# A two-layer transformer block on one core: each change of norm goes by halves of the tokens, and most residual additions go to GpSimd

## The chip, the core and the metric

One core of a Trainium2 chip runs one program in one launch. The time is device microseconds from start to end of that program. The engines are TensorE (PE, matrix products; PEld is its loading of weights), VectorE (DVE), ScalarE (ACT), GpSimd (POOL) and SyncE (SP, which issues loads). They run side by side, each through its own queue in order, and wait for one another only through semaphores. TensorE writes to PSUM, eight banks of 128 x 512 numbers of 32 bits; VectorE and ScalarE read PSUM, and GpSimd works on SBUF.

## What is computed

The input x has 512 tokens of 1024 features. Two layers follow one another. The first mixes tokens by retention (with states of a context of 256 tokens) and by a Fourier transform, and then has a feed-forward part with a convolution along rows of 64 tokens. The second has a causal convolution beside stick-breaking attention, and a gated feed-forward part. Around every part stands the same pattern:

```python
h = modulate(rms_norm(x, g_mix_pre[layer]), sh_a, sc_a)
mix = token_mixer(h, ...)
x = x + gt_a * rms_norm(mix, g_mix_post[layer])
h_ffn = modulate(rms_norm(x, g_ffn_pre[layer]), sh_f, sc_f)
ffn = conv_ffn(h_ffn, ...)
x = x + gt_f * rms_norm(ffn, g_ffn_post[layer])
```

rms_norm divides a token by the root of the mean of its squares. So where one part hands over to the next, each token needs first the mean square of the part's output y, then, with the new x, the mean square of x. The program has three such changes of norm inside it (after the first mixer, after the first feed-forward part, after the second mixer). The last norm, before the output, is made in another way and is not touched.

## The kernel before

**Layout.** Activations lie feature-major: a tile is 128 features by 512 tokens, and a tensor of 1024 features has KT = 8 tiles. All products are in two pieces: weights and activations are split into a rounded part (WH, hH) and the remainder (WL, hL), and `mm3` makes three matmuls of them. Weights come as chunks of 128 x 2048 (SP loads `raw`, ScalarE rounds it to WH in `split_hi`, VectorE makes the remainder WL in `split_lo`), in three slots; the load of chunk c waits until chunk c-3 has been used.

**A stage's end.** `out_phase` (first and third change) and `down_phase` (second) compute the eight tiles of y, two by chunk. For every tile ScalarE takes two squares from PSUM (of y, and of y times the gain gp), and VectorE writes y times gain to yT and its product with x, and adds these three up in `sums` (`out_tile`: four operations, L1164 to L1176). For the last tile VectorE instead makes the product and yT straight from PSUM.

**The change of norm.** `late_stats` adds, on TensorE, the last tile's squares and product to the sums over features (`token_sums`, with a matrix of ones), ScalarE takes the inverse root (`y_root`), VectorE works out from the three sums what the mean square of the new x will be (`boundary`), ScalarE takes its inverse root, and TensorE spreads each root over all partitions (`spread`, L1526). Between these steps `keep_running` (L1780) issues 13 matmuls whose result is not used. Then, for each of eight tiles, VectorE scales y (L1183), adds it to x (L1187), multiplies by gain and root (L1210), ScalarE adds the shift and rounds (hH, L646), and VectorE takes the remainder (hL, L1216). `lead` on TensorE takes these tiles as they come, for two chunks at once: eight matmuls on hH and four on hL each. `third` does the third chunk after that.

**Order.** Nothing is scheduled by a program: each engine's instructions stand in the order written in its block, and the semaphores are counted.

## Time and profile before

| | us |
|---|---|
| time, median of 3 runs (lowest to highest) | 1351.64 (1349.67 to 1352.57) |
| the profiled execution: time / span | 1350.7 / 1348.9 |
| TensorE busy in the span | 1331.0 (99%) |
| VectorE busy | 901.1 (67%) |
| ScalarE busy | 527.0 (39%) |
| GpSimd busy | 84.0 (6%) |
| granted clock of TensorE, mean | 0.999 |

Busy times overlap in a pipelined engine: matmuls of 128 x 512 last 0.39 us each and start 0.227 us apart. So what TensorE costs is read from the starts of its instructions, and what it idles from the numbers in brackets. A time in a timeline is the start from the span's beginning; the number behind it is how long the instruction took.

### The profile page before, as it was taken

Reading aid. Unit: us, or ns where it says so; the run is one execution under the profiler, and the core shown is the slowest. Engines: PE = TensorE matmul, PEld = TensorE weight load, DVE = VectorE, ACT = ScalarE, POOL = GpSimd, SP = SyncE. Lnnn points to the kernel's source line nnn. Section 1 sums busy time; section 2 is a strip of 40 time slices with the busy share of each in tenths; the row PEclk is TensorE's granted clock in tenths of the full one; section 3 lists DMA queues with packets and bytes.
Section 4 is the critical chain, followed back from the end, with each engine's and each line's share of the span. In section 5 each row is a group of like instructions: output and inputs, shape, how many; then the busy total and the mean of one; then the engine's idle time right before and its main releaser. Section 6 shows DMA issues by size and latency. Waiting matters only on the chain.

```text
span 1348.9 us, 15748 instructions
## 1 busy us (share of the span) xinstructions
PE 1331.0 (99%) x6467; PEld 1078.8 (80%) x6467; DVE 901.1 (67%) x1126; ACT 527.0 (39%) x747; POOL 84.0 (6%) x148
## 2 busy tenths in 40 slices
PE   7999999999999999999999999999999999999998
PEld 4799688778888888887888777778878888888886
DVE  4787878988777777678758799766775333332224
ACT  4552444344344443222422666774333222222112
POOL 0000001000000001000000100000001220000000
PEclk9999999999999999999999999999999999999999
DMA  9543046325445455664122211112224332224321
GB/s 387 193 139 127 17 155 218 126 78 176 166 160 201 172 185 179 213 212 162 71 94 97 91 63 63 63 63 95 95 81 139 115 113 98 94 95 162 109 104 63
DMA packets 32887, 176.47 MB, mean 131 GB/s; under 512 B 4128, under 2 KB 4400, under 8 KB 17840
## 3 DMA queue, kind: packets, MB, share of 16 engines
q1 hardware_dynamic: 19440, 128.78, 26.7%
q0 software_dynamic: 13376, 46.69, 10.7%
q8 instruction: 51, 0.84, 0.2%
q14 instruction: 20, 0.16, 0.0%
HBM read 171.26 MB, written 4.20 MB: 130 GB/s over the span
## 4 chain that ended last, share of the span: by engine, by line
PE 90%; DVE 5%; ACT 2%; DMA 1%; issue 1%; SPq 0%; DVEq 0%; ACTq 0%
PE bank L1473 27%; PE bank L1475 26%; PE bank L1474 26%; PE bank L1813 2%; PE bank L1814 2%; PE bank L1819 2%; PE bank L1678 1%; DMA adaf<-ada 1%; DVE WL L829 1%; PE bank L2018 1%; PE bank L1988 1%; PE bank L2006 1%; DVE sums L1172 1%; PE bank L2005 1%; DMA raw<-weights 0%
## 5 line engine op out<-in xcount | busy, mean ns | idle before, releaser
L1473 PE MATMUL bank<-hH,WH 128*128 128x512 f32 x992 | 390.0, 393 | 0.9 <-DVE WL L829 0.6
L829 DVE TENSOR_TENSOR WL<-raw,WH 128x2048 fp32r<-128x2048 f32 x103 | 234.5, 2279 | 232.0 <-ACT WH L371 232.0
L1475 PE MATMUL bank<-hH,WL 128*128 128x512 f32 x992 | 386.4, 390 | 0.0
L1474 PE MATMUL bank<-hL,WH 128*128 128x512 f32 x992 | 386.2, 389 | 0.0
L371 ACT ACTIVATE WH<-raw 128x2048 fp32r<-128x2048 f32 x106 | 201.7, 1905 | 245.8 <-DMA raw<-weights 245.8
L1473 PEld LDWEIGHTS bank<-hH,WH 128*128 128x128 f32 x992 | 186.3, 188 | 42.5 <-issue 3.3
L1475 PEld LDWEIGHTS bank<-hH,WL 128*128 128x128 f32 x992 | 186.2, 188 | 39.6
L1474 PEld LDWEIGHTS bank<-hL,WH 128*128 128x128 f32 x992 | 186.3, 188 | 37.6 <-issue 0.2
L858 DVE SCALAR_TENSOR_TENSOR ada_acc<-ada_half,csil,ada_acc 128x1024 f32<-128x1024 f32 x70 | 89.7, 1281 | 6.0 <-DMA ada_half<-ada_later 3.5
L1305 DVE SCALAR_TENSOR_TENSOR cacc<-uT,vec,cacc 128x511 f32<-128x511 f32 (+29 forms) x120 | 83.3, 759 | 0.0
L334 POOL DMA_DIRECT2D ada_half<-ada_later x80 | 42.6, 533 | 574.9 <-DVE ada_acc L858 341.0
L1473 PE MATMUL bank<-GH,WH 128*128 128x512 f32 x176 | 68.8, 391 | 0.0
L1474 PE MATMUL bank<-GL,WH 128*128 128x512 f32 x176 | 68.5, 389 | 0.0
L1475 PE MATMUL bank<-GH,WL 128*128 128x512 f32 x176 | 68.5, 389 | 0.0
L1473 PE MATMUL bank<-WH,GH 128*128 128x512 f32 x176 | 68.5, 389 | 0.0
L1474 PE MATMUL bank<-WL,GH 128*128 128x512 f32 x176 | 68.5, 389 | 0.0
L1475 PE MATMUL bank<-WH,GL 128*128 128x512 f32 x176 | 68.5, 389 | 0.0
L805 ACT ACTIVATE GH<-tB 128x512 fp32r<-128x512 f32 x22 | 14.0, 634 | 86.8 <-DVE tB L1444 86.8
L1263 DVE SCALAR_TENSOR_TENSOR tB<-bank,vec,tB 128x504 f32<-128x504 f32 x22 | 16.4, 743 | 40.8 <-ACT tB L659 40.7
L659 ACT ACTIVATE tB<-bank,vec 128x512 f32<-128x512 f32 x22 | 17.2, 780 | 67.0 <-PE bank L1475 67.0
L1813 PE MATMUL bank<-hH,WH 128*128 128x512 f32 x96 | 37.6, 392 | 1.8 <-ACT hH L646 1.8
L1473 PEld LDWEIGHTS bank<-GH,WH 128*128 128x128 f32 x176 | 33.0, 188 | 7.1 <-issue 0.2
(333 smaller groups left out, 2080.8 us busy)
## 6 DMA issues: line engine op xcount, KB each, us to landing
raw<-weights SPq DMA_DIRECT2D x108, 1024.0 KB, 4.9
ada_half<-ada_later POOLq DMA_DIRECT2D x80, 512.0 KB, 4.0
adaf<-ada SPq DMA_DIRECT2D x8, 1024.0 KB, 20.0
xT<-x_t SPq DMA_DIRECT2D x4, 512.0 KB, 6.1
x_rows<-xB POOLq DMA_DIRECT2D x32, 64.0 KB, 2.2
x_tok<-x_rows POOLq DMA_DIRECT2D x1, 2048.0 KB, 10.7
out_t<-x_tok SPq DMA_DIRECT2D x8, 256.0 KB, 2.0
ctxT<-ctx_t SPq DMA_DIRECT2D x1, 1024.0 KB, 28.2
```

Of the source, the lines that this page charges most:

```text
L334: pool.dma_start(ada_half[:, a % 2, :], ada_later[a]).then_inc(ada_in[a % 2], 16)
L371: A(WH[:, slot, 0:width], raw[:, slot, 0:width], ACT.Copy).then_inc(s.hi_done, 1)
L659: A(tmp[:, j, :], bank[2 * (t % 3) + x][:, :], ACT.Identity, bias=v("cb", x * FT + t), scale=v("cw", 2 * FT + x * FT + t)).then_inc(s.conv ...
L829: TT_(WL[:, slot, 0:width], raw[:, slot, 0:width], WH[:, slot, 0:width], sub).then_inc(s.lo_done, 1)
L858: ins = STT(ada_acc[:, :], w, c_col, ada_acc[:, :], mult, add)
L1305: STT(cacc[:, k, shift:L], uT[:, k, 0:L - shift], w, cacc[:, k, shift:L], mult, add)\
L1473: mm(o, lh, rh, start=start, stop=False, skip_group_check=skip)
L1474: mm(o, lh, rl, start=False, stop=False, skip_group_check=skip)
L1475: return mm(o, ll, rh, start=False, stop=stop, skip_group_check=skip)
L1813: mm(o, wh, hH[:, k, :], start=(k == 0), stop=False)
L1814: mm(o, wl, hH[:, k, :], start=False, stop=False)
L1819: ins = mm(bank[banks[j] + x][:, :], wh, hL[:, k, :], start=False, stop=(k == KT - 1))
```

## The change

The last two tiles of y (6 and 7) and the first four tiles of the next stage's input are each taken in two halves of 256 tokens. `TURNS` lists the twelve turns: tiles 0 to 3 of the first half, 0 to 3 of the second, then 4 to 7 whole. `closing` on TensorE makes tile 6 and tile 7 on the first half, then both on the second half, and puts the statistics and the spreading of the first half between the products of the second; `lead` starts with the first half and has the statistics of the second half between its products. `keep_running` is gone. ScalarE now takes one square of tiles 6 and 7 and writes y times gain itself; the square with gain comes from the weights of the summing (gp_last has two columns). The split of the second leading chunk is made in two halves (`lead_hi`, `lead_lo`). VectorE makes the addition to x for turns 0, 4 and 8 only; the other nine of each change are made by GpSimd (`residual`). The additions of squares before a stage's last statistics are five instead of six, and the sums are closed at tile 5 instead of tile 6. For the first change `mod_sum` moves ahead of tile 6. PSUM banks are handed out differently, and the three chunks of a column of w_down hold 8, 6 and 8 blocks instead of 8, 8 and 6.

```diff
-Y_BANKS = {0: (2, 3, 0, 1), 1: (2, 3, 0, 1), 2: (0, 1, 2, 3), 3: (2, 3, 0, 1)}
+Y_BANKS = {0: (2, 3, 0, 1), 1: (0, 1, 2, 3), 2: (0, 1, 2, 3)}
+UP_BANKS = (2, 0, 4)
...
+FIRST, SECOND, BOTH = slice(0, HALF), slice(HALF, L), slice(0, L)
+TURNS = [(k, FIRST) for k in range(4)] + [(k, SECOND) for k in range(4)] + [(k, BOTH) for k in range(4, KT)]
+NT = len(TURNS)
+OWN_ADDS = (0, 4, 8)
+DOWN_AT = (0, 8, 14, FT)
...
+            def residual(m):
+
+                for i, (k, ts) in enumerate(TURNS):
+                    if i not in OWN_ADDS:
+                        pool.wait_ge(s.y_scaled, NT * m + i + 1)
+                        nc.gpsimd.tensor_tensor(xT[:, k, ts], xT[:, k, ts], yT[:, k, ts], add).then_inc(s.x_new, 1)
...
                 pool.dma_start(ada_half[:, a % 2, :], ada_later[a]).then_inc(ada_in[a % 2], 16)
+                if a == STEPS_UP + 1:
+                    residual(0)
+
+            residual(1)
...
+            def change(m, c):
+
+                def lead_hi(half):
+                    slot = (c + 2) % SLOTS
+                    at = slice(CH // 2 * half, CH // 2 * half + CH // 2)
+                    if half == 0:
+                        act.wait_ge(raw_in[slot], 16 * ((c + 2) // SLOTS) + 16)
+                    A(WH[:, slot, at], raw[:, slot, at], ACT.Copy).then_inc(s.hi_done if half else s.hi_half, 1)
+
+                def square(n, half):
+                    ts, b = TURNS[4 * half][1], bank[Y_BANKS[m][2 + n]]
+                    act.wait_ge(s.mm_done, done(c, 2 * half + n, 4))
+                    if half == 0:
+                        act.wait_ge(s.sq_added, 5 * m + 4 + n)
+                    A((scratch, odd_sq[m])[n][:, 0, ts], b[:, ts], ACT.Square).then_inc(s.yy_ready, 1)
+
+                def gained(n, half):
+                    ts, b = TURNS[4 * half][1], bank[Y_BANKS[m][2 + n]]
+                    ins = A(yT[:, 6 + n, ts], b[:, ts], ACT.Identity, scale=gp[:, 6 + n:7 + n])
+                    ins.then_inc(s.bank_free if half else s.zz_ready, 1)
...
+                def rounded(i):
+                    k, ts = TURNS[i]
+                    at = SHIFT_AT[m + 1] + k
+                    act.wait_ge(s.norm_mul, KT + NT * m + i + 1)
+                    A(hH[:, k, ts], tmp1[:, k % 4, ts], ACT.Identity, bias=mod[:, at:at + 1]).then_inc(s.h_hi, 1)
+
+                square(0, 0)
+                gained(0, 0)
+                lead_hi(0)
+                square(1, 0)
+                gained(1, 0)
+                y_root(0)
+                square(0, 1)
+                x_root(0)
+                gained(0, 1)
+                rounded(0)
+                square(1, 1)
+                gained(1, 1)
+                rounded(1)
+                y_root(1)
+                rounded(2)
+                rounded(3)
+                x_root(1)
+                rounded(4)
+                rounded(5)
+                lead_hi(1)
+                rounded(6)
+                rounded(7)
+                split_hi(c + 3)
+                for i in range(8, NT):
...
-                if n == KT - 1:
-                    b = bank[Y_BANKS[m][n % 4]]
-                    dve.wait_ge(s.yy_ready, m * KT + n + 1)
-                    STT(last_xy[m][:, :], b[:, :], gp[:, n:n + 1], xT[:, n, :], mult, mult).then_inc(s.xy_ready, 1)
-                    TS(yT[:, n, :], b[:, :], gp[:, n:n + 1], None, mult).then_inc(s.bank_free, 1)
-                    return
-                dve.wait_ge(s.zz_ready, m * (KT - 1) + n + 1)
+                dve.wait_ge(s.zz_ready, 8 * m + n + 1)
...
+            def change(m, c, free0):
+
+                def lead_lo(half):
+                    slot = (c + 2) % SLOTS
+                    at = slice(CH // 2 * half, CH // 2 * half + CH // 2)
+                    if half:
+                        dve.wait_ge(s.hi_done, c + 3)
+                    else:
+                        dve.wait_ge(s.hi_half, 2 + m + 1)
+                    TT_(WL[:, slot, at], raw[:, slot, at], WH[:, slot, at], sub)\
+                        .then_inc(s.lo_done if half else s.lo_half, 1)
...
+                def product(n, half):
+                    ts = TURNS[4 * half][1]
+                    to = scratch[:, 1, ts] if n == 0 else last_xy[m][:, ts]
+                    if half:
+                        dve.wait_ge(s.bank_free, free0 + 7 + n)
+                    else:
+                        dve.wait_ge(s.zz_ready, 8 * m + 7 + n)
+                    TT_(to, yT[:, 6 + n, ts], xT[:, 6 + n, ts], mult).then_inc(s.xy_ready, 1)
...
+                def rest(i):
+                    k, ts = TURNS[i]
+                    at = SHIFT_AT[m + 1] + k
+                    dve.wait_ge(s.h_hi, KT + NT * m + i + 1)
+                    STT(hL[:, k, ts], tmp1[:, k % 4, ts], mod[:, at:at + 1], hH[:, k, ts], add, sub)\
+                        .then_inc(s.h_lo, 1)
+
+                product(0, 0)
+                lead_lo(0)
+                product(1, 0)
...
+                mean_a(0)
+                mean_b(0)
+                dve.wait_ge(s.y_spread, 2 * m + 1)
                 scale_y(0)
+                add_x(0)
                 scale_y(1)
-                add_x(0)
+                product(0, 1)
                 dve.wait_ge(s.gm_ready, m + 1)
-                dve.wait_ge(s.x_spread, m + 2)
...
+                dve.wait_ge(s.x_spread, 2 * m + 2)
+                norm(0)
+                scale_y(2)
+                rest(0)
+                norm(1)
+                scale_y(3)
+                product(1, 1)
+                rest(1)
+                norm(2)
+                mean_a(1)
+                rest(2)
+                norm(3)
+                mean_b(1)
+                rest(3)
+                dve.wait_ge(s.y_spread, 2 * m + 2)
+                scale_y(4)
+                add_x(4)
+                scale_y(5)
+                dve.wait_ge(s.x_spread, 2 * m + 3)
+                norm(4)
+                scale_y(6)
+                rest(4)
+                norm(5)
+                scale_y(7)
+                rest(5)
+                norm(6)
+                lead_lo(1)
+                rest(6)
+                scale_y(8)
+                norm(7)
+                add_x(8)
+                rest(7)
+                scale_y(9)
+                norm(8)
+                dve.wait_ge(s.bank_free, free0 + KT)
+                scale_y(10)
+                rest(8)
+                norm(9)
+                scale_y(11)
+                rest(9)
...
-                pe.wait_ge(s.sq_added, 6 * m + 6)
-                token_sums(4, sums[m][:, 0, :], True, False)
-                token_sums(5, sums[m][:, 1, :], True, False)
-                pe.wait_ge(s.xy_added, 6 * m + 6)
-                token_sums(6, sums[m][:, 2, :], True, False)
-
-            def keep_running(m, times):
-
-                c, still = ((C_UP, mixH[:, 7, :]), (C_U, GH[:, 10, :]), (C_UP2, q2L[:, 3, :]))[m]
-                for _ in range(times):
-                    mm(bank[7][:, :], wblock(c, 0, 0, P)[0], still, start=True, stop=True)
-
-            def late_stats(m):
...
-                have((C_UP, C_U, C_UP2)[m])
+                pe.wait_ge(s.sq_added, 5 * m + 5)
+                token_sums(6, sums[m][:, 0, :], True, False)
                 pe.wait_ge(s.mod_read, (2, 5, 6)[m])
-                keep_running(m, 2)
-
-                pe.wait_ge(s.yy_ready, (m + 1) * KT)
-                token_sums(4, odd_sq[m][:, 0, :], False, True).then_inc(s.ystat_done, 1)
+                token_sums(7, sums[m][:, 1, :], True, False, at=P)
+                pe.wait_ge(s.xy_added, 5 * m + 5)
+                token_sums(6, sums[m][:, 2, :], False, False, at=2 * P)
+
+            def late_squares(m, half):
+
+                qs = (2 * half, 2 * half + 1)
+                pe.wait_ge(s.yy_ready, 10 * m + 8 + 2 * half)
+                token_sums(6, scratch[:, 0, :], False, False, blocks=qs)
...
+            def spread_half(b, src, half):
+
+                ps = slice(64 * half, 64 * half + 64)
+                for q in (2 * half, 2 * half + 1):
+                    ins = mm(bank[b][:, P * q:P * q + P], lift[ps, q:q + 1].to_broadcast([64, P]), src[ps, :],
+                             start=True, stop=True, skip_group_check=True)
+                return ins
+
...
+            def spread_x(m, half):
+
+                pe.wait_ge(s.xroot_ready, 2 * m + half + 2)
+                if half:
+                    pe.wait_ge(s.norm_mul, KT + NT * m + 4)
+                spread_half(5, xroot, half).then_inc(s.x_spread, 1)
...
+            def closing(m, c, ks, src_h, src_l):
+
+                def part(n, half, a, b):
+                    ts, o = TURNS[4 * half][1], bank[Y_BANKS[m][2 + n]]
+                    for x in range(a, b):
+                        kb, k = ks[x]
+                        wh, wl = wblock(c, kb, P * n, P * n + P)
+                        ins = mm3(o[:, ts], wh, wl, src_h[:, k, ts], src_l[:, k, ts],
+                                  m != 1 and half == 0 and x == 0, x == KT - 1, True)
+                    if b == KT:
+                        ins.then_inc(s.mm_done, step(2 * half + n, 4))
+
+                part(0, 0, 0, KT)
+                part(1, 0, 0, 4)
+                early_stats(m)
+                part(1, 0, 4, KT)
+                pe.wait_ge(s.zz_ready, 8 * m + 7)
+                part(0, 1, 0, 3)
+                late_squares(m, 0)
+                part(0, 1, 3, 6)
...
+                late_products(m, 0)
+                spread_y(m, 0)
+                part(0, 1, 6, KT)
+                pe.wait_ge(s.zz_ready, 8 * m + 8)
+                part(1, 1, 0, 5)
+                spread_x(m, 0)
+                part(1, 1, 5, KT)
+
+            def lead(m, c, banks, freed):
+
+                def with_hi(i, js=(0, 1)):
...
+                have(c)
+                pe.wait_ge(s.bank_free, freed - 2)
+                with_hi(0, (0,))
+                with_lo(0, (0,))
+                late_squares(m, 1)
+                with_hi(1, (0,))
+                pe.wait_ge(s.lo_half, 2 + m + 1)
+                pe.wait_ge(s.bank_free, freed)
+                with_hi(0, (1,))
+                with_lo(0, (1,))
+                with_hi(1, (1,))
+                with_lo(1)
+                late_products(m, 1)
+                spread_y(m, 1)
+                with_hi(2)
+                with_lo(2)
+                with_hi(3)
+                spread_x(m, 1)
+                with_lo(3)
+                for i in range(4, NT):
+                    if i == 8:
+                        have(c + 1)
+                    with_hi(i)
+                    with_lo(i)
...
-                        if m == 0 and t == KT - 1:
-                            mod_sum(1, 2)
...
+                if m == 0:
+                    mod_sum(1, 2)
+                closing(m, c0 + 3, order, src_h, src_l)
...
-                        ks = [(k, 8 * j + k) for k in range(min(8, FT - 8 * j))]
+                        ks = [(k, DOWN_AT[j] + k) for k in range(DOWN_AT[j + 1] - DOWN_AT[j])]
```

**TensorE's queue at the end of the first mixer.** `sums`, `odd_sq`, `last_xy` and `scratch` hold the squares and products, `rstd,lift` is the spreading of a root. Before:

```order
L1519 MATMUL bank<-sums_163,ones 32x128 x12
L1473 MATMUL bank<-mixH,WH 128x512
L1474 MATMUL bank<-mixL,WH 128x512
L1475 MATMUL bank<-mixH,WL 128x512
L1780 MATMUL bank<-mixH,WH 128x512 x2
L1519 MATMUL bank<-odd_sq_161,ones 32x128 x4
L1519 MATMUL bank<-odd_sq_161,gp_last 32x128 x4
L1780 MATMUL bank<-mixH,WH 128x512 x2
L1519 MATMUL bank<-last_xy_162,ones 32x128 x4
L1526 MATMUL bank<-rstd,lift 128x128 x4
L1780 MATMUL bank<-mixH,WH 128x512 x4
```

After, from the first half's late statistics to its first spreading:

```order
L1604 MATMUL bank<-mixH,WL 128x256
L1648 MATMUL bank<-scratch,ones 32x128 x2
L1648 MATMUL bank<-odd_sq_161,ones 32x128 x2
L1648 MATMUL bank<-scratch,gp_last 32x128 x2
L1648 MATMUL bank<-odd_sq_161,gp_last 32x128 x2
...
L1604 MATMUL bank<-mixH,WL 128x256
L1648 MATMUL bank<-scratch,ones 32x128 x2
L1648 MATMUL bank<-last_xy_162,ones 32x128 x2
L1929 MATMUL bank<-rstd,lift 128x128 x2
L1602 MATMUL bank<-mixH,WH 128x256
```

The sums and the spreading now stand between products of 256 columns instead of between matmuls without use.

**VectorE's queue before tile 6 of the first mixer.** Before (tile 5, then tile 6):

```order
L1164 TENSOR_SCALAR yT<-bank,gp 128x512
L1167 TENSOR_TENSOR last_xy_162<-yT,xT 128x512
L1172 TENSOR_TENSOR sums_163<-sums_163,odd_sq_161 128x1024
L1176 TENSOR_TENSOR sums_163<-sums_163,last_xy_162 128x512
L1164 TENSOR_SCALAR yT<-bank,gp 128x512
```

After (tile 5, then the first half of tile 6):

```order
L941 TENSOR_TENSOR mod<-bank,vec 128x16
L1220 TENSOR_SCALAR yT<-bank,gp 128x512
L1223 TENSOR_TENSOR last_xy_162<-yT,xT 128x512
L1228 TENSOR_TENSOR sums_163<-sums_163,odd_sq_161 128x1024
L1232 TENSOR_TENSOR sums_163<-sums_163,last_xy_162 128x512
L1253 TENSOR_TENSOR scratch<-yT,xT 128x256
L1243 TENSOR_TENSOR WL<-raw,WH 128x1024
```

The sums that TensorE takes up in tile 7 now end with tile 5's, and the small operation on `mod` stands ahead of them.

**VectorE's queue in the next stage's input.** Before, one tile after another:

```order
L1210 SCALAR_TENSOR_TENSOR tmp_132<-xT,gm,bank 128x512
L1183 TENSOR_TENSOR yT<-yT,bank 128x512
L1187 TENSOR_TENSOR xT<-xT,yT 128x512
L1216 SCALAR_TENSOR_TENSOR hL<-tmp_132,mod,hH 128x512
```

After, turns 6 to 8:

```order
L1285 SCALAR_TENSOR_TENSOR tmp_132<-xT,gm,bank 128x256
L1243 TENSOR_TENSOR WL<-raw,WH 128x1024
L1292 SCALAR_TENSOR_TENSOR hL<-tmp_132,mod,hH 128x256
L1273 TENSOR_TENSOR yT<-yT,bank 128x512
L1285 SCALAR_TENSOR_TENSOR tmp_132<-xT,gm,bank 128x256
L1278 TENSOR_TENSOR xT<-xT,yT 128x512
L1292 SCALAR_TENSOR_TENSOR hL<-tmp_132,mod,hH 128x256
L1273 TENSOR_TENSOR yT<-yT,bank 128x512
L1285 SCALAR_TENSOR_TENSOR tmp_132<-xT,gm,bank 128x512
```

The split of half a chunk and three whole-width operations stand between the half-width ones that TensorE's turns 6 to 8 wait for.

## Rows read from the trace of the kernel before

**Rows 1.** The page's slices, tenths busy of TensorE and its granted clock, whole run.

```profile
PE   7999999999999999999999999999999999999998
...
PEclk9999999999999999999999999999999999999999
```

**Rows 2.** Timeline of PE, first change: start us, us, engine line op, idle before.

```profile
253.02 0.39 PE L1473 MATMUL bank<-mixH,WH 128*128 128x512 f32 x1
...
258.74 0.50 PE L1473 MATMUL bank<-mixH,WH 128*128 128x512 f32 x1
...
265.09 0.40 PE L1475 MATMUL bank<-mixH,WL 128*128 128x512 f32 x1
...
266.40 0.43 PE L1519 MATMUL bank<-odd_sq,ones 128*32 128x128 f32 x8
266.64 0.40 PE L1519 MATMUL bank<-odd_sq,gp_last 128*32 128x128 f32 x8
...
270.25 1.16 PE L1526 MATMUL bank<-rstd,lift 128*128 128x128 f32 x8 [0.16 <-ACT rstd L382]
271.16 1.41 PE L1780 MATMUL bank<-mixH,WH 128*128 128x512 f32 x5
273.16 0.47 PE L1813 MATMUL bank<-hH,WH 128*128 128x512 f32 x1 [0.59 <-ACT hH L646]
...
295.01 0.39 PE L1473 MATMUL bank<-hH,WH 128*128 128x512 f32 x1
```

**Rows 3.** Timeline of PE, second and third change.

```profile
633.15 1.03 PE L1519 MATMUL bank<-sums,ones 128*32 128x128 f32 x24 [0.52 <-DVE sums L1172]
...
634.69 0.40 PE L1475 MATMUL bank<-GH,WL 128*128 128x512 f32 x1
...
642.53 0.47 PE L1813 MATMUL bank<-hH,WH 128*128 128x512 f32 x1 [0.60 <-ACT hH L646]
...
976.48 0.40 PE L1475 MATMUL bank<-mgH,WL 128*128 128x512 f32 x1
...
984.32 0.47 PE L1813 MATMUL bank<-hH,WH 128*128 128x512 f32 x1 [0.60 <-ACT hH L646]
```

**Rows 4.** Timeline of PE, 256-column products of an early stage.

```profile
74.01 0.28 PE L1475 MATMUL bank<-WH,hL 128*128 128x256 f32 x1
74.13 0.28 PE L1473 MATMUL bank<-WH,hH 128*128 128x256 f32 x1
```

**Rows 5.** Timeline of DVE, first change and, last row, before the third.

```profile
258.39 1.22 DVE L1172 TENSOR_TENSOR sums<-sums,odd_sq 128x1024 f32<-128x1024 f32 x1
...
271.51 0.75 DVE L1210 SCALAR_TENSOR_TENSOR tmp<-xT,gm,bank 128x512 f32<-128x512 f32 x1 [0.30 <-PE bank L1526]
...
971.68 0.75 DVE L1164 TENSOR_SCALAR yT<-bank,gp 128x512 f32<-128x512 f32 x1 [2.11 <-ACT scratch L607]
```

**Rows 6.** Timeline of ACT: a 512-column rounding at the first change, a 256-column one early.

```profile
272.29 0.72 ACT L646 ACTIVATE hH<-tmp,mod 128x512 fp32r<-128x512 f32 x1 [2.10 <-DVE tmp L1210]
...
63.65 0.51 ACT L377 ACTIVATE hcH<-tmpc,mod 128x256 fp32r<-128x256 f32 x1 [0.27 <-DVE tmpc L888]
```

**Rows 7.** Timeline of DVE: 256-column operations elsewhere.

```profile
63.13 0.48 DVE L888 SCALAR_TENSOR_TENSOR tmpc<-ctxT,gm,crstd 128x256 f32<-128x256 f32 x1
63.53 0.49 DVE L893 SCALAR_TENSOR_TENSOR hcL<-tmpc,mod,hcH 128x256 fp32r<-128x256 f32 x1
...
794.01 0.76 DVE L1347 TENSOR_TENSOR spL<-spF,spH 128x256 fp32r<-128x256 f32 x2
```

**Rows 8.** Timeline of POOL, additions of 128x256, then of DVE beside the second pair.

```profile
771.18 4.33 POOL L343 TENSOR_TENSOR spF<-spF,spF 128x256 f32<-128x256 f32 x2 [5.66 <-DVE spL L1347]
...
803.50 2.12 POOL L343 TENSOR_TENSOR spF<-spF,spF 128x256 f32<-128x256 f32 x2 [7.99 <-DVE spL L1347]
...
801.19 1.37 DVE L1305 SCALAR_TENSOR_TENSOR cacc<-uT,vec,cacc 128x491 f32<-128x491 f32 x2
...
803.81 1.22 DVE L1305 SCALAR_TENSOR_TENSOR cacc<-uT,vec,cacc 128x491 f32<-128x491 f32 x1
```

271 lines of the change are left out of this document (128 added, 143 removed).

## The prediction

> **What bounds the kernel now.** I read the page first. TensorE is at nine tenths or more in nearly every slice and its clock is fully granted throughout [rows 1], so the time is the number of matmuls times their spacing, plus the places where TensorE does nothing useful. The timeline of TensorE around the three changes of norm shows these. At the first, the last product starts at 265.09 and the next stage's first matmul at 273.16 [rows 2]. Products start 0.227 us apart (tile 6 runs from 253.02 to 258.46, 24 products), so the gap is 273.16 - 265.32 = 7.84 us. At the second and third it is 642.53 - 634.92 = 7.61 and 984.32 - 976.71 = 7.61 [rows 3]. The second also has 0.5 us of waiting for VectorE's sums before it [rows 3]. The gaps hold 23.1 us, 23.6 with that wait: this is what the change can touch. In a gap nothing is slow for lack of an engine. It is one chain: sums, root, mean, root, spreading, first tile.
>
> **What TensorE has to do in place of the gap.** For each change:
> - Products by halves. In closing 2 tiles x 2 halves x 8 blocks x 3 = 96, in the lead 8 turns x 12 = 96. A 256-column product with new weights takes 74.13 - 74.01 = 0.120 us [rows 4], against half of 0.227 = 0.1134. 192 x 0.0066 = 1.3 us.
> - Sums over features: 16 for squares and 8 for products, each (266.64 - 266.40) / 4 = 0.06 [rows 2]: 1.4 us.
> - Spreading: 8 matmuls at (271.16 - 270.25) / 4 = 0.228 [rows 2]: 1.8 us. That they now contract over 64 partitions has no row; I take the same.
> - Switching between products and these small ones. The first product after four others lasts 0.50 instead of 0.39 [rows 2]; I take 0.1 in and 0.1 out, at six places: 1.2 us.
>
> Together 5.7 us, with no wait anywhere. The saving would be 7.84 - 5.7 = 2.1 at the first change, 7.61 + 0.5 - 5.7 = 2.4 at the second, 1.9 at the third: 6.4 us at the very most. The 13 idle matmuls cost nothing extra when they go, since they filled waiting.
>
> **The waits that the halves bring.** I walked the four queues of the new program with durations from the rows.
> - *First change, the early sums.* Tile 6 still starts at 253.02; mod_sum, moved ahead, costs 0.4 (258.74 - 258.46 and the longer product after it); 36 half products take 4.3. TensorE asks for the sums at 257.7. They must now include tile 5, whose addition of squares starts at 258.39 and takes 1.22 [rows 5]; with the small operation on mod in front, about 0.2, it ends at 259.8. Before, the sums up to tile 6 were asked for six microseconds later. Wait: 2.1 us. At the third change VectorE has idled 2.11 us before tile 6 [rows 5], so it isn't behind; at the second there are two whole chunks in between. No wait there.
> - *First half's chain.* The whole chain that took 7.84 now runs beside 48 half products (5.8 us) and 2.9 us of sums and spreading, so most of it hides. At its end: spreading to VectorE's start took 271.51 - 270.25 = 1.26 with four matmuls [rows 2, 5], so 0.80 with two; the multiplication 0.48 [rows 7]; ScalarE 0.03 later, 0.51 [rows 6]; TensorE 0.15 after ScalarE (272.29 + 0.72 to 273.16) [rows 2, 6]. That is 1.97, and TensorE has 0.46 + 0.1 + 9 x 0.12 = 1.64 to do. Wait 0.35. Turns 1 and 3 add about 0.3 between them.
> - *Second half's root.* The same 1.97, but only four matmuls of turn 3 (0.48) stand behind the spreading: 1.97 - 1.04 = 0.9.
> - *No lead builds up.* A half turn is 12 x 0.12 = 1.44 on TensorE. VectorE's loop per turn, with ScalarE's rounding inside it, is 0.48 + 0.03 + 0.51 + 0.03 + 0.40 = 1.45 [rows 6, 7] (0.40 is 63.53 - 63.13). So whatever else stands in VectorE's queue here is paid in full.
> - *Turn 7.* Between the multiplications of turns 6 and 7 stand the half split (1.22 for 1024 columns [rows 5], spaced 1.13), a remainder (0.40) and a whole-width scaling (about 0.60, half of what 1024 columns take): 2.53 against 1.44, and 0.15 more on the remainder: 1.25.
> - *Turn 8.* Between 7 and 8 stand 0.40 + 0.60 + 0.40 + 0.60 = 2.0, and the whole-width multiplication and rounding take 0.75 + 0.72 instead of 0.48 + 0.51 [rows 5, 6]: 2.5 against 1.44, so 1.05. From there on whole tiles (2.72) outlast the loop again.
>
> Sum of the waits in each change: 0.35 + 0.3 + 0.9 + 1.25 + 1.05 = 3.9 us, and 2.1 more in the first.
>
> **GpSimd's additions.** 27 additions leave VectorE: 18 of 256 columns (about 0.33, from 0.76 for two [rows 7]) and 9 of 512 (0.60). Most fall into pauses while VectorE waits for ScalarE, so little is gained by them; in my walk they are gone already. On GpSimd an addition of 128x256 took 2.12 / 2 = 1.06, and for the first pair 4.33 beside a 2048-wide split [rows 8]; at 512 no row shows it, and I take twice, 2.1. The additions are issued one or two turns ahead, so that length mostly hides. What doesn't: VectorE's operation with two SBUF inputs took 1.22 beside GpSimd, where two such alone took 1.37, 0.69 each [rows 8]. The remainder (tmp and hH, both in SBUF) is such an operation and overlaps the addition. Bounds: 0 if they miss each other, 0.5 for each half turn and 1.0 for each whole if they meet fully. I take 0.2 per half turn, as they overlap by about a third; carried through the loop it makes 1.0 us per change.
>
> By the Trainium skill, GPSIMD Engine Reference, section 3.1, an addition costs about 2.6 cycles of 1.2 GHz per element, which would be an estimated 0.55 us for 256 columns. The row shows 1.06, so here I go by the row. With the page's figure the additions would be over sooner and the 1.0 us might vanish, giving about 1359.
>
> What else moves costs nothing that I can find: ScalarE's share of work is small (it is busy for 39% of the span), the split of the third chunk is done long before TensorE gets to it, the chunks of 8, 6 and 8 blocks give each load as much cover as 8, 8, 6, and the loads through GpSimd's queue wait behind the additions only when two buffers are full.
>
> **The sum.** First change: -2.1 + 2.1 + 3.9 + 1.0 = +4.9. Second: -2.4 + 3.9 + 1.0 = +2.5. Third: -1.9 + 3.9 + 1.0 = +3.0. Together +10.4 us. On the profiled execution, 1350.7, that is 1361.1; on the median, 0.9 higher, **1362.0**. With the prices a little off either way: 1357 to 1367.
>
> **Rivals.**
> 1. *VectorE and ScalarE keep ahead of TensorE, and the kernel gets faster.* It needs a loop under about 1.2 us per half turn, so that some 1.2 us of lead stands when the half split comes. Then turns 7 and 8 and the small waits vanish, and only the 2.1 us of the first change stays: -6.4 + 2.1 = -4.3, 1347.3. For it: the 256-column durations come from other stages. Against it: 0.48, 0.51 and 0.40 repeat there without exception. Chance 0.13.
> 2. *Half of the waits.* The walk overstates handovers and switching: 1349 to 1357. Chance 0.10, with 0.06 of it within 0.2%.
> 3. *GpSimd holds VectorE fully.* Each remainder loses 0.5 or 1.0: by the same walk +3.2 more per change, 1372. For it: the 1.22 [rows 8], and the first pair of additions, which stood still beside the split. Against it: they overlap only partly. The Trainium skill, SBUF — State Buffer, section "SBUF: two separate sides", says the shared pair of ports is held exclusively for a whole instruction; that rule gives this case. Chance 0.10.
> 4. *The clock falls.* keep_running is gone, and TensorE waits up to 2.1 us. If after each change some 10 us ran at 1.2 instead of 2.4 GHz, each would cost about 5 us more: 1377. The trace shows full clock also in the first slice, where TensorE is busy for only seven tenths [rows 1]. The Trainium skill, TensorE: Matmul & The Clock Gate, Part 1, says the default is the lower clock and activity releases it; the first slice doesn't show that. Chance 0.05.
>
> **How the numbers follow.** The forecast has 0.62. A measurement here tells about 0.2% from nothing, 2.7 us. Faster than that: rival 1 and a little of 2, 0.14. Within: 0.06. Slower: 0.80. The range 1349 to 1373 leaves out rival 1 below and rival 4 above, 0.18 in all.
>
> **What would show it.** Right: no gap after the last product, but brackets before the hH matmuls of turns 0, 4, 7 and 8 with ScalarE's rounding as releaser, of 0.3, 0.9, 1.1 and 1.0 us, at all three changes; a bracket of about 2 us with VectorE's sums in tile 7 of the first; half products at 0.120; from the start of tile 6 to the third chunk's first matmul 47 us in the first change, where it was 295.01 - 253.02 = 42.0 [rows 2]. Wrong: half turns at 1.44 us without brackets (rival 1); remainders of 0.9 us and more (rival 3); a granted clock under 1 (rival 4).

## Result and profile after

The changed kernel takes 1368.47 us (median of 4 runs, 1367.9 to 1372.42), the kernel before 1350.68 in the same comparison (1349.67 to 1352.57). The ratio is 1.0136, interval 1.0113 to 1.0159: slower, and by 17.8 us where 10.4 were forecast. The profiled execution took 1368.29 with a span of 1366.5, 17.6 more than the span before.

The page of the changed kernel, where [rows 1] stood before. TensorE is as full as it was and its clock is fully granted:

```profile
PE 1342.8 (98%) x6788; PEld 1096.4 (80%) x6788; DVE 903.8 (66%) x1159; ACT 537.9 (39%) x789; POOL 108.8 (8%) x175
...
PE   7999999999999999999999999999999999999998
...
PEclk9999999999999999999999999999999999999999
```

So the slices don't show where the time went. The timeline of TensorE does. Here is the second change, from the first half product of tile 6 to the first matmul of the third chunk (what was [rows 3] before):

```profile
629.14 0.28 PE L1602 MATMUL bank<-GH,WH 128*128 128x256 f32 x1
...
637.05 0.41 PE L1648 MATMUL bank<-scratch,ones 128*32 128x128 f32 x4
637.29 0.39 PE L1648 MATMUL bank<-odd_sq,ones 128*32 128x128 f32 x4
...
638.04 0.39 PE L1602 MATMUL bank<-GH,WH 128*128 128x256 f32 x1
...
645.20 0.36 PE L1985 MATMUL bank<-hH,WH 128*128 128x256 f32 x1
...
655.59 0.39 PE L1985 MATMUL bank<-hH,WH 128*128 128x256 f32 x1 [0.64 <-ACT hH L686]
...
656.65 0.64 PE L1994 MATMUL bank<-hL,WH 128*128 128x256 f32 x4
657.41 0.39 PE L1985 MATMUL bank<-hH,WH 128*128 128x256 f32 x1
...
660.28 0.68 PE L1994 MATMUL bank<-hL,WH 128*128 128x256 f32 x4
661.74 0.39 PE L1985 MATMUL bank<-hH,WH 128*128 128x256 f32 x1 [0.79 <-ACT hH L686]
661.97 0.28 PE L1986 MATMUL bank<-hH,WL 128*128 128x256 f32 x1
...
664.36 0.47 PE L1985 MATMUL bank<-hH,WH 128*128 128x512 f32 x1 [0.92 <-ACT hH L686]
...
676.18 0.39 PE L1602 MATMUL bank<-hH,WH 128*128 128x512 f32 x1
```

There is no gap after the last product any more. In its place stand pauses before turns 4 (655.59), 7 (661.74) and 8 (664.36). Some have no bracket: from 656.65 to 657.41 four matmuls should take 0.48 and took 0.76. And a half product that follows a bracketed pause or a group of small matmuls starts the next one 0.22 to 0.23 later instead of 0.12 (661.74 to 661.97).

Read so at all three changes, the stretch from the end of tile 5 to the third chunk splits in two. *Closing* ends at the first hH matmul, *lead* ends at the third chunk (us; the second change of before has 12 whole products, 2.72 us, added to it, since the changed kernel's last chunk holds 8 blocks and not 6):

| | first: closing + lead | second | third |
|---|---|---|---|
| before | 20.14 + 21.85 | 20.26 + 21.88 | 19.49 + 21.85 |
| after | 18.27 + 30.80 | 16.06 + 30.98 | 16.06 + 30.80 |
| difference | +7.1 | +4.9 | +5.5 |

The sum is 17.5 us, all of the 17.6. The closing gave back 1.9 to 4.2 us, the lead took 9.0.

VectorE and GpSimd in turns 4 to 6 of the second change. First VectorE: the remainder (hL), then gain and root (tmp), scaling, and the next remainder.

```profile
655.57 0.85 DVE L1292 SCALAR_TENSOR_TENSOR hL<-tmp,mod,hH 128x256 fp32r<-128x256 f32 x1 [0.24 <-ACT hH L686]
656.34 0.47 DVE L1285 SCALAR_TENSOR_TENSOR tmp<-xT,gm,bank 128x256 f32<-128x256 f32 x1
656.74 0.41 DVE L1273 TENSOR_TENSOR yT<-yT,bank 128x256 f32<-128x256 f32 x1
657.39 0.85 DVE L1292 SCALAR_TENSOR_TENSOR hL<-tmp,mod,hH 128x256 fp32r<-128x256 f32 x1 [0.25 <-ACT hH L686]
...
658.55 1.21 DVE L1243 TENSOR_TENSOR WL<-raw,WH 128x1024 fp32r<-128x1024 f32 x1
659.69 0.47 DVE L1292 SCALAR_TENSOR_TENSOR hL<-tmp,mod,hH 128x256 fp32r<-128x256 f32 x1
```

Then GpSimd's additions in the same stretch:

```profile
655.41 0.73 POOL L341 TENSOR_TENSOR xT<-xT,yT 128x256 f32<-128x256 f32 x1 [0.22 <-DVE yT L1273]
657.22 0.73 POOL L341 TENSOR_TENSOR xT<-xT,yT 128x256 f32<-128x256 f32 x1 [1.08 <-DVE yT L1273]
```

A remainder that begins inside an addition takes 0.85; with none beside it, at 659.69, it takes 0.47. The addition ends at 656.14 and the remainder at 656.42, 0.28 later. So it did most of its work only once GpSimd was done. In each change this happens to six of the twelve remainders: those of turns 0, 1, 4 and 5, and the whole ones of turns 8 and 9, which take 1.72 instead of 0.75. The other six meet no addition.

### The profile page after: what moved, and what is told of

Read it like the earlier page. It is cut to its first block, busy times and chain, and to the rows that moved or that the text cites. A ratio compares the mean times of both kernels' runs of the same rounds, so it can differ in the third digit from the quotient of the medians.

```text
span 1366.5 us, 16514 instructions
## 1 busy us (share of the span) xinstructions
PE 1342.8 (98%) x6788; PEld 1096.4 (80%) x6788; DVE 903.8 (66%) x1159; ACT 537.9 (39%) x789; POOL 108.8 (8%) x175
## 3 DMA queue, kind: packets, MB, share of 16 engines
q0 software_dynamic: 13376, 46.69, 10.4%
## 4 chain that ended last, share of the span: by engine, by line
PE 88%; DVE 5%; ACT 3%; issue 2%; DMA 1%; SPq 0%; DVEq 0%; ACTq 0%
PE bank L1602 27%; PE bank L1604 26%; PE bank L1603 26%; DMA adaf<-ada 1%; PE bank L1807 1%; ACT hH L686 1%; PE bank L2210 1%; PE bank L1648 1%; DVE tmp L1285 1%; PE bank L1985 1%; ACT WH L389 1%; PE bank L2180 1%; PE bank L1994 1%; DVE hL L1292 1%; PE bank L1986 1%
## 5 line engine op out<-in xcount | busy, mean ns | idle before, releaser
L1602 PE MATMUL bank<-hH,WH 128*128 128x512 f32 x992 | 390.1, 393 | 0.7 <-DVE WL L891 0.5
L891 DVE TENSOR_TENSOR WL<-raw,WH 128x2048 fp32r<-128x2048 f32 x100 | 227.6, 2278 | 232.7 <-ACT WH L389 232.6
L389 ACT ACTIVATE WH<-raw 128x2048 fp32r<-128x2048 f32 x103 | 195.8, 1903 | 238.3 <-DMA raw<-weights 238.2
L1602 PE MATMUL bank<-GH,WH 128*128 128x512 f32 (+1 forms) x192 | 71.9, 375 | 0.0
L1603 PE MATMUL bank<-GL,WH 128*128 128x512 f32 (+1 forms) x192 | 71.3, 371 | 0.0
L1604 PE MATMUL bank<-GH,WL 128*128 128x512 f32 (+1 forms) x192 | 71.3, 371 | 0.0
L1985 PE MATMUL bank<-hH,WH 128*128 128x256 f32 (+1 forms) x144 | 45.9, 340 | 8.1 <-ACT hH L686 6.8
L1986 PE MATMUL bank<-hH,WL 128*128 128x256 f32 (+1 forms) x144 | 42.9, 319 | 0.0
```

What stands on the lines that cost most here:

```text
L389: A(WH[:, slot, 0:width], raw[:, slot, 0:width], ACT.Copy).then_inc(s.hi_done, 1)
L891: TT_(WL[:, slot, 0:width], raw[:, slot, 0:width], WH[:, slot, 0:width], sub).then_inc(s.lo_done, 1)
L1602: mm(o, lh, rh, start=start, stop=False, skip_group_check=skip)
L1603: mm(o, lh, rl, start=False, stop=False, skip_group_check=skip)
L1604: return mm(o, ll, rh, start=False, stop=stop, skip_group_check=skip)
L1985: mm(o, wh, hH[:, k, ts], start=(i == 0), stop=False, skip_group_check=True)
```

## Experiments

Each kernel ran beside the kernel before. Times are medians; experiment 5 is a single run.

**1. All additions on VectorE.**

```diff
-OWN_ADDS = (0, 4, 8)
+OWN_ADDS = tuple(range(NT))
...
                 norm(4)
                 scale_y(6)
+                add_x(5)
                 rest(4)
```

> The changed kernel with all twelve additions of each change of norm on VectorE, each put into a pause in which VectorE waits for ScalarE; halves and everything else as they are. Theory (GpSimd's additions hold VectorE's remainders, nothing else does): the remainders of turns 0, 1, 4, 5 fall from 0.85 to 0.48 us and those of turns 8 and 9 from 1.72 to 0.75. By the walk with the durations of the changed kernel's trace, the lead shrinks from 30.84 to 29.18 us, so 1.66 less per change, 5.0 in all: 1363.5. The waits before turns 4 (1.0), 7 (1.1) and 8 (1.1) stay. Rival A (the remainders are slow because of the half size, or because ScalarE works beside them): they stay at 0.85 and VectorE has 3 us of additions more per change: 1368 to 1372. Rival B (most of the loss comes from GpSimd): 1355 or less.

Measured 1364.86, ratio to before 1.0108 (1.0091 to 1.0125). That is 3.6 us less than the changed kernel, where 5.0 were expected. All remainders are fast again (0.48 and 0.75 us in the mean), so rival A is out, and rival B's 1355 is far off. The leads are 29.24, 29.61 and 29.25 us, where 29.18 was expected, and the first and third closing are 0.2 and 0.3 longer than in the changed kernel, probably because VectorE now has the additions in its own queue.

**2. The additions stay on GpSimd, at another time.**

```diff
                         pool.wait_ge(s.y_scaled, NT * m + i + 1)
+                        if i >= 2:
+                            pool.wait_ge(s.h_lo, KT + NT * m + i - 1)
```

> The changed kernel; the additions stay on GpSimd, but the addition of turn i also waits until the remainder of turn i-2 is done, so that it runs between two remainders instead of beside one. Theory (an overlap in time holds VectorE, GpSimd's work itself costs nothing): remainders at 0.48 and 0.75 us throughout, the lead 1.8 us shorter in each change, 5.5 in all: 1363.0. Rival (remainders are slow for another reason than the overlap): no change, 1368.5. Second rival (the additions then come too late for the multiplications by gain and root, which wait for them): slower than 1368.5.

Measured 1363.53, ratio 1.0093 (1.0078 to 1.0108). The groups of remainders (count, busy us, mean ns), of the changed kernel:

```profile
L1292 DVE SCALAR_TENSOR_TENSOR hL<-tmp,mod,hH 128x256 fp32r<-128x256 f32 x24 | 16.2, 676 | 2.4 <-ACT hH L686 2.2
L1292 DVE SCALAR_TENSOR_TENSOR hL<-tmp,mod,hH 128x512 fp32r<-128x512 f32 x12 | 14.8, 1234 | 5.9 <-ACT hH L686 5.9
...
L341 POOL TENSOR_TENSOR xT<-xT,yT 128x256 f32<-128x256 f32 x18 | 13.5, 751 | 181.8 <-DVE yT L1273 181.7
L341 POOL TENSOR_TENSOR xT<-xT,yT 128x512 f32<-128x512 f32 x9 | 11.5, 1285 | 20.4 <-DVE yT L1273 20.4
```

and of the second experiment:

```profile
L1294 DVE SCALAR_TENSOR_TENSOR hL<-tmp,mod,hH 128x256 fp32r<-128x256 f32 x24 | 11.6, 482 | 2.4 <-ACT hH L688 2.2
L1294 DVE SCALAR_TENSOR_TENSOR hL<-tmp,mod,hH 128x512 fp32r<-128x512 f32 x12 | 9.0, 752 | 5.9 <-ACT hH L688 5.9
```

The same additions, of the same length, on the same engine cost 4.9 us less when they run between two remainders. So what costs is the overlap, not the work. While they run, VectorE scales y and multiplies by gain and root. Both have one input in PSUM, and both keep their durations (0.48 and 0.41 us at 256 columns). The timelines of the third change, VectorE and then GpSimd:

```profile
998.34 0.48 DVE L1287 SCALAR_TENSOR_TENSOR tmp<-xT,gm,bank 128x256 f32<-128x256 f32 x1
998.74 0.41 DVE L1275 TENSOR_TENSOR yT<-yT,bank 128x256 f32<-128x256 f32 x1
999.40 0.48 DVE L1294 SCALAR_TENSOR_TENSOR hL<-tmp,mod,hH 128x256 fp32r<-128x256 f32 x1 [0.25 <-ACT hH L688]
999.80 0.48 DVE L1287 SCALAR_TENSOR_TENSOR tmp<-xT,gm,bank 128x256 f32<-128x256 f32 x1
...
1001.81 1.50 DVE L1245 TENSOR_TENSOR WL<-raw,WH 128x1024 fp32r<-128x1024 f32 x1
```

```profile
1000.03 0.74 POOL L343 TENSOR_TENSOR xT<-xT,yT 128x256 f32<-128x256 f32 x1 [0.83 <-DVE hL L1294]
1001.49 0.74 POOL L343 TENSOR_TENSOR xT<-xT,yT 128x256 f32<-128x256 f32 x1 [0.72 <-DVE hL L1294]
```

One addition now meets the split of the leading chunk (two inputs in SBUF), which takes 1.50 where it took 1.21 in the changed kernel. TensorE then waits 0.21 to 0.22 us for the remainder of turn 6 in each change, a wait that the changed kernel doesn't have; this can be the 0.5 us by which the run missed its number.

The Trainium skill, SBUF — State Buffer, section "SBUF: two separate sides", says that an operation of VectorE with two SBUF inputs and one of GpSimd share a pair of ports, which the one that starts first keeps to its end. The traces agree, for 0.85 and 1.72 against 0.48 and 0.75. The trace of the kernel before shows the other direction too. These are the two additions of the second pair in [rows 8], and VectorE's operation ahead of them (two rows in one, until 803.90):

```profile
803.50 1.00 POOL L343 TENSOR_TENSOR spF<-spF,spF 128x256 f32<-128x256 f32 x1 [7.99 <-DVE spL L1347]
804.46 1.17 POOL L343 TENSOR_TENSOR spF<-spF,spF 128x256 f32<-128x256 f32 x1
...
802.87 1.03 DVE L1347 TENSOR_TENSOR spL<-spF,spH 128x384 fp32r<-128x384 f32 x2
```

Each addition began inside an operation of VectorE with two SBUF inputs and ended 0.60 after it: 804.50 after 803.90, and 805.63 after 805.03 (the operation at 803.81 in [rows 8]). So GpSimd is held as well when VectorE was first; an addition of this size takes 0.73 us in the changed kernel with nothing of the kind ahead of it.

**3. The additions on GpSimd alone, in whole tiles.** The kernel before, with this for tiles 1 to 7 (k is the tile) in place of VectorE's additions (that of tile 0 stays on VectorE, ahead of the scaling of tile 1):

```diff
+                for k in range(1, KT):
+                    pool.wait_ge(s.y_scaled, KT * m + k + 1)
+                    nc.gpsimd.tensor_tensor(xT[:, k, :], xT[:, k, :], yT[:, k, :], add).then_inc(s.x_new, 1)
```

> The kernel before, in whole tiles, with the additions of tiles 1 to 7 on GpSimd in all three changes: the one part of the change without the other. Theory (an addition of 512 columns takes 1.28 us and holds the remainder beside it for 0.97): the loop of a tile becomes 0.66 + 0.03 + 0.72 + 0.03 + 1.72 = 3.17 us where TensorE needs 2.72; six turns are held, 6 x 0.45 = 2.7 us per change, 8 in all: 1358.8. Rival (the additions on GpSimd cost nothing by themselves, the halves make all of the loss): 1350.7.

Measured 1358.4, ratio 1.0057 (1.0042 to 1.0072). The timeline of VectorE, third change: one tile takes 996.90 - 993.73 = 3.17, of which the remainder is 1.72. It ends at 996.98, 0.54 after GpSimd's addition (the last row).

```profile
993.73 0.74 DVE L1221 SCALAR_TENSOR_TENSOR tmp<-xT,gm,bank 128x512 f32<-128x512 f32 x1
994.39 0.68 DVE L1194 TENSOR_TENSOR yT<-yT,bank 128x512 f32<-128x512 f32 x1
995.26 1.72 DVE L1225 SCALAR_TENSOR_TENSOR hL<-tmp,mod,hH 128x512 fp32r<-128x512 f32 x1 [0.20 <-ACT hH L657]
996.90 0.73 DVE L1221 SCALAR_TENSOR_TENSOR tmp<-xT,gm,bank 128x512 f32<-128x512 f32 x1
...
995.15 1.29 POOL L334 TENSOR_TENSOR xT<-xT,yT 128x512 f32<-128x512 f32 x1 [1.88 <-DVE yT L1194]
```

**4. The same with the later start.** Again one wait more: the addition of tile k also waits for the remainder of tile k-2.

> The kernel before with the additions of tiles 1 to 7 on GpSimd, and that of tile k waiting also for the remainder of tile k-2. Theory (only the overlap with the remainder costs): all remainders at 0.75 us, no wait in the lead, the time of the kernel before: 1350.8. Rival (the additions on GpSimd cost something beyond that, by their length of 1.28 us in the chain of a tile): up to 1358.4, as without the wait.

Measured 1350.69, ratio 1.0000 (0.9991 to 1.0009). With the start in the right place the additions on GpSimd cost nothing: the remainders take 0.75 us in the mean again, and the leads 21.85 to 21.88. They gain nothing either: in the kernel before, VectorE takes 2.52 us for a tile with its addition (one multiplication by gain and root starts at 645.92, the next at 648.44), less than TensorE's 2.72.

**5. What a sum over features costs.** The closing and the lead of the changed kernel hold more small matmuls than I had paid for: 637.05 to 637.29 above is 0.24 us for two sums, where [rows 2] show 0.24 for four.

```diff
-                for _ in range(times):
-                    mm(bank[7][:, :], wblock(c, 0, 0, P)[0], still, start=True, stop=True)
+                for i in range(4 * times):
+                    q = i % (1, 2, 4)[m]
+                    mm(bank[7][32 * q:32 * q + 32, 0:P], ones[:, 0:32], sums[m][:, 0, 0:P], ...)
```

> A measurement inside the kernel before: each of the 13 idle matmuls in a change of norm is replaced by four sums over features (128x32 weights of ones, 128 columns, result not used). In the first change all four write the same 32 partitions of the bank, in the second they alternate between two quarters, in the third they go through all four. Theory (sums on different quarters of the array run side by side, each takes 0.23 us by itself; this is why two sums of a half take as long as four of a whole tile): four sums take 0.91 us in the first change, 0.46 in the second, 0.23 in the third. Rival (a sum costs 0.06 wherever it writes, and the half's 0.23 is a price for changing between inputs): 0.24 in all three.

One run: 1358.91. The timeline of TensorE, in each of the three changes the four idle matmuls between the spreadings, now 16 sums (32 rows, as a sum is recorded as two):

```profile
270.52 3.68 PE L1780 MATMUL bank<-sums,ones 128*32 128x128 f32 x32
...
645.20 1.94 PE L1780 MATMUL bank<-sums,ones 128*32 128x128 f32 x32
...
988.25 1.08 PE L1780 MATMUL bank<-sums,ones 128*32 128x128 f32 x32
```

A row's length holds the end of its last sum, and a single sum is recorded with about 0.28 us. From first start to last start there are 15 steps: (3.68 - 0.28) / 15 = 0.23, then 0.11 and 0.05 us. So four sums take about 0.9, 0.44 and 0.21: each needs 0.23 by itself, and those that write different quarters of the partitions run side by side. A half of the tokens writes two quarters only, so its two sums take as long as a whole tile's four. The Trainium skill, TensorE: Matmul & The Clock Gate, "Part 3: Packing small matmuls", describes this for outputs of 32 partitions; the rows agree.

**6. The walk's waits taken away.** Experiment 2, and these moves:

```diff
-                early_stats(m)
+                if m:
+                    early_stats(m)
                 part(1, 0, 4, KT)
+                if m == 0:
+                    early_stats(m)
...
                 gained(1, 0)
+                lead_hi(1)
                 y_root(0)
...
+                lead_lo(1)
                 mean_a(0)
```

(lead_hi(1) and lead_lo(1) go from their places in turns 5 and 6. VectorE's product of a first half also waits until the sums have been read, `xy_added`.)

> The changed kernel with GpSimd's additions moved between the remainders, and two more edits: in the first change the early sums stand after the first half of tile 7 instead of after its fourth block, and both pieces of the second leading chunk are split before the first root, in a pause of ScalarE and VectorE, instead of the second piece between turns 6 and 7. Theory (the waits are what the walk says they are): the early sums' wait falls from 1.6 to 0.2 us, the wait before turn 7 from 1.1 to 0.6 and the small one in turn 6 goes, 0.6 less in each change; against the run with the additions alone moved (1363.5) 1.4 + 3 x 0.6 = 3.2 us: 1360.3. Left are the waits before turn 4 (1.0) and turn 8 (1.1). Rival (a wait only moves to the next turn, since VectorE's loop is as long as TensorE's): 1362.

Measured 1360.26, ratio 1.0071 (1.0058 to 1.0085). The first closing is 1.44 shorter than the changed kernel's (16.55 against 17.99, both without mod_sum), the leads are 28.42 to 28.46. The early sums' wait is 0.18, the bracket before turn 7 is 0.35 instead of 0.79.

**7. Half sums in four quarters.** Experiment 6, and the sums of squares with gain of a half go to the free quarters:

```diff
+                    for q in qs:
+                        y = token_sums(6, sq[:, 0, :], False, n == 1, blocks=(q,))
+                        z = token_sums(7, sq[:, 0, :], False, n == 1, by, P, (q,), 2)
```

(The early sums with gain move by two quarters too, and VectorE reads them there.)

> The run with the additions, the early sums and the splits moved (1360.3), with one more edit: of a half's sums, those of squares with gain go to the two quarters of their bank that the half leaves free, and the eight are issued in turn with those of plain squares, so that four write four different quarters. Theory (two sums of 128x32 on two quarters take as long as four on four, 0.23 us): the eight sums take 0.47 instead of 0.93, 0.46 less at two places in each change, 2.8 in all, a little less where VectorE's chain then waits for something else: 1357.6 to 1358.5. Rival (TensorE works them off one after the other, whatever they write): 1360.3.

Measured 1357.26, ratio 1.0053 (1.0037 to 1.0068). The eight sums of a half, the first of their 16 rows and the product behind them:

```profile
976.78 0.30 PE L1652 MATMUL bank<-scratch,ones 128*32 128x128 f32 x1
...
977.36 0.39 PE L1605 MATMUL bank<-mgH,WH 128*128 128x256 f32 x1
```

From the first sum to the product behind is 0.58, where the changed kernel has 638.04 - 637.05 = 0.99. Three waits for ScalarE's rounding are left in brackets in the lead of the third change: 0.45 us before turn 4, 0.36 before turn 7 and 0.93 before turn 8.

**8. Whole tiles, with less in the products' way.** The kernel before, its early sums behind the last product (in `down_phase` too, and VectorE's product of the last tile also waits until the sums have been read, `xy_added`):

```diff
-                            project(o, c0 + p, n, src_h, src_l, order[:-1], True, False)
-                            early_stats(m)
-                            project(o, c0 + p, n, src_h, src_l, order[-1:], False, True)\
-                                .then_inc(s.mm_done, step(n, 2))
+                            project(o, c0 + p, n, src_h, src_l, order).then_inc(s.mm_done, step(n, 2))
...
-                keep_running(m, 2)
-
+                early_stats(m)
                 pe.wait_ge(s.yy_ready, (m + 1) * KT)
```

> The kernel before in whole tiles, with one move: the 12 early sums stand after tile 7's last product, in place of the first two idle matmuls, instead of ahead of its last three products. Theory (the 0.85 us in which TensorE waits for ScalarE's square hides them): 0.9 to 1.0 us of sums and switching leave the products' way, 0.2 comes back behind them; 0.7 less in the first and third change, 1.2 in the second, where the wait of 0.5 for VectorE's last sums goes too: 2.6 us, 1348.2. Rival (the sums end later than the square, and the chain behind them is what counts): no change, 1350.8.

Measured 1350.0, ratio 0.9998 (0.9989 to 1.0007): a miss. In the third change 0.65 us went (18.84 instead of 19.49 up to the first hH matmul), where 0.7 were expected; in the first 0.19 and in the second 0.06. In the first TensorE now waits for VectorE's split of the next chunk, which the sums had stood ahead of before. In the second the same split holds VectorE when the last tile's product is due. TensorE in the first change:

```profile
265.36 0.86 PE L1520 MATMUL bank<-sums,ones 128*32 128x128 f32 x24 [1.08 <-DVE WL L829]
```

and VectorE in the second:

```profile
633.23 2.28 DVE L829 TENSOR_TENSOR WL<-raw,WH 128x2048 fp32r<-128x2048 f32 x1
635.43 0.74 DVE L1161 SCALAR_TENSOR_TENSOR last_xy<-bank,gp,xT 128x512 f32<-128x512 f32 x1
```

**9. Only where it helps.** The move in the first and third change, ahead of the wait for the chunk.

> The kernel before, with the early sums after the last product in the first and third change alone, and there ahead of the wait for the next chunk's remainder. In the run that moved them everywhere the third change got 0.63 us shorter, the first only 0.19, since TensorE waited 1.08 us for VectorE's split of the next chunk, and the second 0.04, since that split (2.28 us) held the product of the last tile. Theory (these two waits took the gain): the first change now gets 0.9 shorter, the third 0.6, the second stays as before: 1.5 us less than before, ratio 0.999. Rival (the first change's chain is held by VectorE's split and the small operation on mod anyway): 0.8 less.

Measured 1349.44 (11 runs), ratio 0.9987 (0.9979 to 0.9996). Up to the first hH matmul the first change is 19.20 us (20.14 before), the third 18.84 (19.49). That is 0.94 and 0.65, where 0.9 and 0.6 were expected. This version is faster than both kernels, by little.

**10. No idle matmuls.** Experiment 8 without keep_running.

> The same as the run with the sums after the last product, without the 11 idle matmuls that are left in each change. Theory (they only fill waiting, and TensorE's clock doesn't depend on them here, as it stayed fully granted in the changed kernel, which has none): same time, 1348.2, granted clock 0.99 or more. [...] Second rival (an idle matmul that has begun delays the spreading behind it): 0.1 to 0.2 us faster for each spreading, 1347.5.

Measured 1353.69, ratio 1.0034 (1.0022 to 1.0046), 3.7 us slower than with them. The busy time of TensorE by stretches in the second change (window, length, busy, granted clock):

```profile
632.00:636.00 4.00, 3.22 (x49) 1.00 0.29 59
636.00:638.00 2.00, 0.82 (x9) 0.82 0.93 393
638.00:640.00 2.00, 1.81 (x8) 0.50 0.03 12
...
642.00:644.00 2.00, 0.25 (x2) 0.50 0.00 0
...
646.00:648.00 2.00, 2.00 (x8) 0.62 0.00 0
648.00:650.00 2.00, 2.00 (x10) 1.00 0.00 0
```

The granted clock is 1.00 up to 636 and 0.82 in the mean of the next 2 us, in which TensorE is busy for 0.82 us. From 638 on it is at half (1.2 GHz). It is still at half when the lead begins at 643.96, and full from 648. It fell in the first change too, after two waits of 1.12 and 1.75 us (0.51 from 272 to 274), and not in the third. With idle matmuls it stayed at 1.00 through the same stretches.

The theory was wrong, then: the time is lost where the clock fell. In the second the closing is 0.9 us longer than in experiment 8 and the lead 1.7. In the first the lead is 1.5 longer, while the closing is 0.3 shorter. In the third, where the clock stayed full, both take what they took with idle matmuls (18.84 and 21.86).

## Why the prediction was right, and where it wasn't

The direction and the mechanism held: one chain's gap was traded for more work on TensorE and for waits in a loop that is no faster than TensorE. The sum was 7.4 us short on the median: TensorE's work was 3.3 us larger per change than forecast, the pauses 0.7 smaller (4.15 against 3.9 + 1.0), and the early sums' wait 0.5 smaller, 3 x (3.3 - 0.7) - 0.5 = 7.3 us. So errors of both signs partly cancelled. The narrow bounds, 1357 to 1367, missed the 1368.47; the range held because it reached up to rival 3. Point by point, for one change:

- **The gap** of 7.6 to 7.8 us went, as said.
- **TensorE's own work, 5.7 forecast.** This is the term that was mis-sized most. In the third change the stretch grew by 5.5. The pauses that can be read in it are 4.15 (turn 0: 0.16 and 0.24; turns 4 to 10: 0.61, 0.28, 0.27, 0.94, 1.09, 0.25, 0.31). So about 7.6 + 5.5 - 4.15 = 9.0 us of work stand in the gap's place. Half products at 0.120 were right (1.3). *Sums at 0.06 each, 1.4,* was the wrong step: 0.06 is a quarter of what four side by side take. 12 calls at 0.23 are 2.8 (experiments 5 and 7). *Switching, 1.2,* was too low as well. From the last product before a group of small matmuls to the second product behind it, less two spacings of 0.12, the trace has 1.19 us for the sums of squares of a half, 1.39 for its sums of products with the first spreading, and 0.83 for the second spreading. Twice that is 6.8, where I had 4.4 for sums, spreading and switching. The sums explain 1.4 of the difference; the other 1.0 is switching, or spreading that costs more between products, which no run here separates. Each of nine pauses costs about 0.1 more at its end, 0.9. That makes 1.3 + 6.8 + 0.9 = 9.0. Without pauses it would be 8.1, against a gap of 7.6 to 8.1 with VectorE's wait: even then the halves could have gained nothing.
- **The early sums of the first change:** 2.1 forecast, 1.62 in a bracket.
- **Waits of the halves, 3.9 forecast.** Without GpSimd in the way (experiment 2, third change) the pauses before turns 4, 7 and 8 are 0.6, 0.95 and 1.08, against 0.9, 1.25 and 1.05, and small ones add 0.6: 3.2. Right in place, somewhat large in size. VectorE's loop took 1.46 us there (999.80 - 998.34), against 1.45. Experiment 6 took away the two waits it aimed at, by what the walk had said.
- **GpSimd beside the remainder, 1.0 forecast, 1.4 to 1.6 measured.** The stretch of the third change is 46.86 after and 45.43 in experiment 2, and 4.9 us of the median are 1.6 per change. Here rival 3 was the true mechanism where the two meet: the remainder is held until the addition ends, and loses 0.37 to 0.46 us at 256 columns and 0.97 at 512, near the 0.5 and 1.0 of that rival. But only six of the twelve meet an addition, 3.5 us of holding in all, and part of that hides. The additions were also shorter than I took them from [rows 8], 0.75 and 1.28 us instead of 1.06 and 2.1, since those of [rows 8] were held themselves (experiment 2). By the figure of the Trainium skill, GPSIMD Engine Reference, section 3.1, I had estimated 0.55; the trace lies between.
- **Rivals 1 and 2** fell: no lead built up, since VectorE's loop never got under TensorE's 1.44.
- **Rival 4,** the clock: it stayed full. But a full first slice was no argument against it, and "the 13 idle matmuls cost nothing extra when they go" holds only with something in their place. Experiment 10 shows the clock fall after waits of 1 to 2 us with little between. In the changed kernel, where half products stand there, it stayed full; without them the idle matmuls of the kernel before are worth 3.7 us.
- **What would show it.** Brackets at turns 4, 7 and 8, as said, but smaller: 0.64, 0.79 and 0.92 in the second change, and only 0.45 at turn 4 in the other two, where 0.9, 1.1 and 1.0 were forecast. There is none at turn 0, where 0.3 was forecast. From the end of tile 5 to the third chunk it took 49.1 us in the first change, where 47 were forecast.

In sum, the experiments account for the 17.8 us so: GpSimd's timing 4.9, the early sums and the splits 3.3, half sums on two quarters 3.0, and 6.4 are left in experiment 7. That adds up to 17.6; the other 0.2 is how far the medians of the kernel before differ between the comparisons. What makes up these 6.4 I read only from the traces: the three pauses named there, and the work of sums, spreading and switching.

## What to carry to other kernels

A gap made of one chain can be filled by cutting the work in two, but the second half pays for every fixed price again: here 9.0 us of half products, small matmuls, switching and restarts stood in for a gap of 7.6. Price each small instruction from a row in which it stands as it will stand: four side by side tell nothing of two. Before moving work to GpSimd, look what VectorE will run at the same instant: one wait that shifted the additions decided between +7.6 us and nothing in the same kernel.

## What was not expected of the hardware

- A remainder with two inputs in SBUF that begins inside GpSimd's addition ends 0.28 us after it at 256 columns and 0.54 at 512: 0.85 instead of 0.48 us, 1.72 instead of 0.75. An addition that begins inside such an operation of VectorE ends 0.60 after that. VectorE's operations with one input in PSUM kept their 0.48 and 0.41 us beside an addition.
- Two sums with 128x32 weights on two quarters take as long as four on four (0.23), and sixteen in a row on one quarter take 3.7.
- TensorE's clock fell to half in a change of norm in two of three places as soon as the idle matmuls were gone, and the run was 3.7 us longer.
- A product of 256 columns after a bracketed pause or after small matmuls starts the next one 0.22 to 0.23 us later, not 0.12.
